# Branch products in three terms of rounded operands, in a mixer and mixture-of-experts kernel

## The chip, the cores and the metric

The kernel runs on one core of one Trainium2 chip. The metric is the device time of one execution in microseconds, the median of several runs. TensorE (PE) multiplies matrices, VectorE (DVE), ScalarE (ACT) and GpSimd (POOL) work on elements, SyncE (SP) issues most transfers. Each engine takes its instructions in the order written; between engines semaphores order the work.

## The reference

One layer for 512 tokens of width 1024. The input goes through one wide projection into four attention branches of four heads (A forgetting, B sliding window, C differential, D dilated) and into four gates of width 1024. The mixer's output is, cut to what matters:

```
for i, y in enumerate((ya, yb, yc, yd)):          # each [512, 256]
    merged = merged + sigmoid(gates[:, :, i]) * (y @ w_branch[i])
return merged @ w_out
```

Branch C is normalised by its mean square over each head before that. Behind the mixer come a layer norm, a router that picks 8 of 64 experts for a token, the experts and a shared one, and a second layer norm. All arrays are float32.

## The kernel before

**Stages.** First the projections and the attention, then mixing (`w_out`), router, 64 experts one after another with weights streamed from memory, and the sum. The change lies in the first stage, which ends near 496 us. SyncE issues the loads of all that follows (`x_nat`, the shared and the experts' weights) only after the last branch product and the last addition, since their memory is that of the attention.

**Rounded operands.** A large product is made of three: every operand is split in a high part, rounded to the type float32r by a ScalarE copy, and a low part, the remainder (GpSimd or VectorE subtracts). The product is high x high + high x low + low x high, all float32r. The branch products alone, of those in this stage with a large weight, use plain float32.

**Weights.** They come in chunks through a ring of three slots (`chunk`, L494 on): 22 chunks of eight 128x128 blocks for projections, then 32 chunks of ten blocks, one for each merge step: eight for a piece of the gate, two of `w_branch`. `split(n)` of ScalarE (L1053) copies the eight gate blocks of chunk n to `w_hi`, `split(n)` of GpSimd (L1649) makes `w_lo`; both have two buffers. SyncE waits, before it loads a slot again, for the remainder of a projection's chunk, or for the branch product of a merge's chunk, as that product reads the slot.

**A merge step m** (32 of them, eight to a branch, one for each 128 columns of the output): `part` 3m to 3m+2 are the three terms of the gate product, each eight matmuls of 128x512 (L680). `gate` is ScalarE's tanh of it (L1130); behind it in ScalarE's queue stands the split of chunk 22+m+2. `branch` is the branch product (L789), two float32 matmuls from `w` in the ring and the turned output `yT`. `gated` is VectorE's (tanh + 1) x product (L1386), and GpSimd adds it to `mT` (L1672).

**The order** of the work is one list, made by `order_of_work`, that every engine walks through. Attention steps (scores, bias, exponential, transpose, values) stand between the parts of merge steps: two steps in each of merges 0 to 5 and 14 to 21, four in each of merges 6 to 13, of branch C. Merges 22 to 31 have none between. In the first kind the list reads `part part, step, part gate branch, step, gated`, in the second `part, step, part, step, part gate, step, branch, step, gated`.

**Turned outputs.** When the last step of a branch is done, `turn_y` (two for a branch, L769) transposes its output on TensorE, and ScalarE copies it to `yT` with a factor of one half (L1124). For branch C the output is first normalised: VectorE's sums (L1349 to L1352), a root on GpSimd (`root`, L1647), VectorE's scaling (`norm_c`, L1362). GpSimd's root stands in its queue behind its split in merge 15. Transposes take two banks in turn, and wait for the copy out of the bank two before.

**w_out**, 4 MB, goes over the first 8192 elements of `region1`. It is issued after chunk 48, whose own wait is for 24 branch products.

```
elif kind == "branch":                              # TensorE
    w = ring[:, j % RING, :].rearrange("p (c n) -> p c n", c=10)
    for c in range(2):
        mm = nc.tensor.matmul(PS[:, C_BANK + 1, :], w[:, KT + c, :], yT[:, (br % 2) * 2 + c, :], ...)
```

Of the kernel before, what the change touches and what calls it, by code (L numbers as in the profile page):

```python
# [26 lines left out]
F32 = mybir.dt.float32  # L27
# [178 lines left out]
def build(nc, a, out):  # L206
# [9 lines left out]
    with ctx:  # L216
# [55 lines left out]

        x_hi = sb1("x_hi", [P, KT, SEQ], F32R)
        x_lo = sb1("x_lo", [P, KT, SEQ], F32R)
        w_hi = sb1("w_hi", [P, HALVES, KT, P], F32R)
        w_lo = sb1("w_lo", [P, HALVES, KT, P], F32R)
        ring = sb1("ring", [P, RING, SLOT])
        region1 = sb1("region1", [P, 29190])

        def carve(region, start, shape):  # L280
            n = int(np.prod(shape))
# [17 lines left out]
        kD, o = carve(region1, o, (2, SEQ))  # L299
        V, o = carve(region1, o, (QT, 7, P))  # L300
        probs, o = carve(region1, o, (3, SEQ + 2))
        probsT, o = carve(region1, o, (3, SEQ))
        Y, o = carve(region1, o, (2 * QT, F))
        yT, o = carve(region1, o, (4, SEQ))
        gate, o = carve(region1, o, (2, SEQ))
        gated, o = carve(region1, o, (2, SEQ))
        assert o == 29190, o
# [20 lines left out]
        for b in range(2):  # L328
            landing = ExitStack()
            raw[b] = landing.enter_context(nc.sbuf_tensor(f"raw{b}", [P, GU + DN], F32))  # L330
            landing.close()
            w_lo_e[b] = sb(f"w_lo_e{b}", [P, GU + DN], F32R)
            if b == 0:

                first = ExitStack()
                first.enter_context(nc.sbuf_tensor("x_nat_from", [P, GU + DN - QT * D], F32))
# [76 lines left out]
        yc_stat = sem("yc_stat")  # L413
        yc_rms = sem("yc_rms")
        y_ready = sem("y_ready")
        gate_done = sem("gate_done")
        gate_tanh = sem("gate_tanh")
        branch_done = sem("branch_done")
# [71 lines left out]
        def _(sp):  # L490
            def chunk(j):
                if j >= RING:

                    if j - RING < N_PROJ:  # L494
                        sp.wait_ge(w_lo_made, j - RING + 1)
                    else:
                        sp.wait_ge(branch_done, j - RING - N_PROJ + 1)
                src, n = (a["w_proj"][j], KT * P) if j < N_PROJ else (a["w_merge"][j - N_PROJ], 10 * P)
                sp.dma_start(ring[:, j % RING, 0:n], src).then_inc(ring_in[j % RING], 16)

# [43 lines left out]
            for j in range(12, N_CHUNKS):  # L544
                chunk(j)
                if j == W_OUT_AFTER:

                    sp.wait_ge(scores_done, last_step[BR_C] + 1)
                    sp.dma_start(w_out, a["w_out"][0].rearrange("(k p) n -> p k n", p=P)).then_inc(w_out_in, 16)


# [85 lines left out]
        def _(pe):  # L637
# [47 lines left out]
            def x_product(bank, n):  # L685
# [10 lines left out]
                    mm = x_product_part(bank, n, i)  # L696
                return mm

            for kind, n in order:
                if kind == "proj":  # L700
                    u = n
# [23 lines left out]
                elif kind == "turn":  # L725
                    u = turn_at[kind, n]
                    br, _, _, qt = STEPS[n]
                    if br == BR_C:
                        pe.wait_ge(combined, (n - FIRST_C) // 2 + 1)
                    else:  # L730
                        pe.wait_ge(probs_made, n + 1)
                    if u >= 2:
                        pe.wait_ge(turned_out, u - 1)
                    else:
                        pe.wait_ge(forget_exp, 1)
                    for j in range(keys_of(br, qt)[1]):
                        mm = nc.tensor.transpose(PS[:, T_BANK + u % 2, j * P:(j + 1) * P],  # L737
                                                 probs[:, n % 3, j * P:(j + 1) * P], ident[:, :])
                    mm.then_inc(turned, 1)
                elif kind == "turn_v":  # L740
                    u = turn_at[kind, n]
                    pe.wait_ge(proj_out, n + 1)
                    if u >= 2:
                        pe.wait_ge(turned_out, u - 1)
                    else:
                        pe.wait_ge(forget_exp, 1)
                    for t in range(QT):
                        mm = nc.tensor.transpose(PS[:, T_BANK + u % 2, t * P:(t + 1) * P],
                                                 vT[:, V_AT[PROJ[n][1:]] % 2, t * P:(t + 1) * P], ident[:, :])
                    mm.then_inc(turned, 1)  # L750
                elif kind == "values":
                    br, _, _, qt = STEPS[n]
                    k0, nk = keys_of(br, qt)
                    need = max(m for m, x in enumerate(PROJ) if x[1] == br and x[0] == "v")
                    pe.wait_ge(turned_out, max(turn_at["turn", n], turn_at["turn_v", need]) + 1)
                    v = VALUE_AT[n]
                    if v >= 2:
                        pe.wait_ge(y_made, v - 1)
                    for j in range(nk):
                        mm = nc.tensor.matmul(PS[:, O_BANK + v % 2, 0:HD], probsT[:, v % 3, j * P:(j + 1) * P],  # L760
                                              v_of(n, k0 + j), start=(j == 0), stop=(j == nk - 1))
                    mm.then_inc(values_done, 1)
                elif kind == "turn_y":
                    u = turn_at[kind, n]
                    br, j = n // 2, n % 2
                    pe.wait_ge(y_ready, br + 1)
                    pe.wait_ge(turned_out, u - 1)
                    for t in range(QT):
                        mm = nc.tensor.transpose(PS[:, T_BANK + u % 2, t * P:(t + 1) * P],  # L769
                                                 Y[:, (br % 2) * QT + t, j * P:(j + 1) * P], ident[:, :])  # L770
                    mm.then_inc(turned, 1)
                elif kind == "part":
                    m, i = divmod(n, 3)
                    if i == 0:
                        if m == 0:
                            pe.wait_ge(proj_out, N_PROJ)
                        else:
                            pe.wait_ge(gate_tanh, m)
                    mm = x_product_part(C_BANK, N_PROJ + m, i)
                    if i == 2:  # L780
                        mm.then_inc(gate_done, 1)
                elif kind == "branch":
                    j, br = N_PROJ + n, n // KT
                    w = ring[:, j % RING, :].rearrange("p (c n) -> p c n", c=10)
                    pe.wait_ge(turned_out, turn_at["turn_y", 2 * br + 1] + 1)
                    if n >= 1:
                        pe.wait_ge(gated_made, n)
                    for c in range(2):
                        mm = nc.tensor.matmul(PS[:, C_BANK + 1, :], w[:, KT + c, :], yT[:, (br % 2) * 2 + c, :],  # L789
                                              start=(c == 0), stop=(c == 1))  # L790
                    mm.then_inc(branch_done, 1)


# [19 lines left out]
            def turn_x1(t):  # L813
                pe.wait_ge(x1_made, t + 1)
                if t == 0:
                    pe.wait_ge(turned_out, len(turns))
                else:
                    pe.wait_ge(x1T_made, t)
                xs = x1[:, t, :].rearrange("p (q c) -> p c q", c=KT)
# [225 lines left out]
        def _(act):  # L1045
# [7 lines left out]
            def split(n):  # L1053

                if n < N_CHUNKS:
                    act.wait_ge(ring_in[n % RING], 16 * (n // RING + 1))
                    nc.scalar.activation(w_hi[:, n % HALVES, :, :],  # L1057
                                         ring[:, n % RING, 0:KT * P].rearrange("p (c n) -> p c n", c=KT), ACT.Copy)\
                        .then_inc(w_hi_made, 1)

            split(0)
# [13 lines left out]
            for kind, n in order:  # L1075
# [42 lines left out]
                elif kind == "turn_y":  # L1118
# [5 lines left out]
                    nc.scalar.activation(yT[:, (br % 2) * 2 + j, :], PS[:, T_BANK + u % 2, :], ACT.Copy, scale=0.5)\  # L1124
                        .then_inc(turned_out, 1)
                elif kind == "gate":
                    act.wait_ge(gate_done, n + 1)
                    if n >= 2:
                        act.wait_ge(gated_made, n - 1)
                    nc.scalar.activation(gate[:, n % 2, :], PS[:, C_BANK, :], ACT.Tanh, scale=0.5)\  # L1130
                        .then_inc(gate_tanh, 1)
                    split(N_PROJ + n + HALVES)

            def x1T_copy(t):
# [115 lines left out]
        def _(dve):  # L1250
# [117 lines left out]
            for kind, n in order:  # L1368
# [3 lines left out]
                        norm_c()  # L1372
                elif kind == "join":
                    combine(n)
                elif kind == "values":
                    out_step(n)
                elif kind == "gated":
# [244 lines left out]
        def _(pool):  # L1622
# [25 lines left out]

            def split(n):  # L1649

                w = ring[:, n % RING, 0:KT * P].rearrange("p (c n) -> p c n", c=KT)
                wh, wl = w_hi[:, n % HALVES, :, :], w_lo[:, n % HALVES, :, :]
# [134 lines left out]
```

## Time and profile before

| | us |
|---|---|
| median of 3 runs (lowest to highest) | 1338.59 (1338.19 to 1339.23) |
| the profiled execution, its own time | 1335.51 |
| its span in the profile | 1333.9 |
| TensorE busy | 1265.3 (95%) |
| VectorE busy | 779.1 (58%) |
| ScalarE busy | 706.6 (53%) |
| GpSimd busy | 386.9 (29%) |
| mean TensorE clock granted | 0.981 of full |

The span is the time from the first to the last instruction in the profile; the profiled execution's own time holds a little around it, and it is 3 us under the median of the runs. A busy share is a mean over stages that are limited by different things. The end of a matmul is modelled and matmuls overlap, so their price is read from starts: where one group starts and where the next one does.

### The profile page before, as it was taken

How to read it: one execution, taken by the hardware profiler on the slowest of the kernel's cores; microseconds unless marked ns; L12 is line 12 of the kernel's file. 1: busy time of each engine (PE TensorE's matmuls, PEld its weight loads, DVE VectorE, ACT ScalarE, POOL GpSimd, SP SyncE). 2: the span in 40 equal slices, each digit the busy share in tenths (PEclk: the TensorE clock that was granted, in tenths of full speed). 3: DMA queues.
4: the chain of work that ended last, by engine and by line, in shares of the span. 5: the costliest groups of instructions: out<-in, count | busy, mean ns of one | idle time of the engine just before them, and what ended most of it. 6: DMA issues, size and time to landing. Idle time of an engine off the chain costs nothing.

```text
span 1333.9 us, 14628 instructions
## 1 busy us (share of the span) xinstructions
PE 1265.3 (95%) x5488; PEld 919.0 (69%) x5488; DVE 779.1 (58%) x1071; ACT 706.6 (53%) x854; POOL 386.9 (29%) x262
## 2 busy tenths in 40 slices
PE   7999999999999999969999999999999999999965
PEld 4888866566667764444887777777777777777722
DVE  4011122344422014642888888888888888887858
ACT  4333433333333210011778888887888888887710
POOL 3433322223333430253332322223223223233201
PEclk9999999999999999979999999999999999999978
DMA  4922112111112515042899999999999999999686
GB/s 160 324 85 80 59 45 74 40 59 60 40 66 73 205 43 226 1 159 82 323 378 380 373 367 374 370 376 357 363 375 375 368 361 375 363 370 371 250 333 250
DMA packets 68118, 311.28 MB, mean 233 GB/s; under 512 B 17788, under 2 KB 17916, under 8 KB 41552
## 3 DMA queue, kind: packets, MB, share of 16 engines
q1 hardware_dynamic: 48560, 276.64, 56.0%
q0 software_dynamic: 19488, 33.70, 6.7%
q8 instruction: 45, 0.74, 0.2%
q14 instruction: 25, 0.20, 0.0%
HBM read 305.74 MB, written 42.01 MB: 261 GB/s over the span
## 4 chain that ended last, share of the span: by engine, by line
PE 61%; DMA 25%; ACT 5%; DVE 5%; issue 2%; POOL 1%; another core or an unknown queue 1%; SPq 0%; POOLq 0%; DVEq 0%; ACTq 0%
DMA raw<-in_w_gu 23%; PE PS L680 22%; PE PS L926 8%; PE PS L789 4%; PE PS L876 4%; ACT w_hi_e L1156 4%; PE PS L723 4%; PE PS L879 3%; PE PS L873 3%; PE PS L807 3%; PE PS L760 2%; PE PS L737 2%; DMA parts<-y_d 1%; PE PS L858 1%; PE PS L907 1%
## 5 line engine op out<-in xcount | busy, mean ns | idle before, releaser
L1475 DVE TENSOR_TENSOR w_lo_e<-raw,w_hi_e 128x2048 fp32r<-128x2048 f32 x192 | 433.8, 2283 | 5.0 <-ACT w_hi_e L1156 5.0
L1156 ACT ACTIVATE w_hi_e<-raw 128x2048 fp32r<-128x2048 f32 x192 | 368.4, 1920 | 111.6 <-DMA raw<-in_w_gu 70.0
L1703 POOL DMA_INDIRECT y_d<-y_slots,tab x64 | 113.6, 1776 | 425.6 <-PE PS L945 305.8
L1655 POOL TENSOR_TENSOR w_lo<-ring,w_hi 128x1024 fp32r<-128x1024 f32 x54 | 128.3, 2376 | 309.3 <-ACT w_hi L1057 309.3
L1318 DVE CUSTOM_DVE_ANT_0 region<-PS,region 128x128 f32<-128x128 f32 (+3 forms) x64 | 31.4, 491 | 211.6 <-PE PS L723 210.1
L876 PE MATMUL PS<-w_hi_e,xs_lo 128*128 128x512 f32 x512 | 144.5, 404 | 0.0
L873 PE MATMUL PS<-w_hi_e,xs_hi 128*128 128x512 f32 x512 | 143.8, 402 | 0.0
L879 PE MATMUL PS<-w_lo_e,xs_hi 128*128 128x512 f32 x512 | 138.7, 393 | 0.0
L1100 ACT ACTIVATE region<-region,nmax 128x128 f32<-128x128 f32 (+5 forms) x80 | 43.6, 545 | 139.8 <-DVE nmax L1318 139.6
L876 PEld LDWEIGHTS PS<-w_hi_e,xs_lo 128*128 128x128 f32 x512 | 91.7, 188 | 33.4 <-DVE xs_lo L1501 16.0
L680 PE MATMUL PS<-x_hi,w_hi 128*128 128x512 f32 x424 | 112.8, 408 | 0.0
L879 PEld LDWEIGHTS PS<-w_lo_e,xs_hi 128*128 128x128 f32 x512 | 96.1, 188 | 22.3
L680 PE MATMUL PS<-x_hi,w_lo 128*128 128x512 f32 x432 | 110.4, 398 | 0.0
L680 PE MATMUL PS<-x_lo,w_hi 128*128 128x512 f32 x424 | 105.7, 391 | 0.0
L873 PEld LDWEIGHTS PS<-w_hi_e,xs_hi 128*128 128x128 f32 x512 | 91.5, 189 | 15.6 <-issue 0.5
L680 PEld LDWEIGHTS PS<-x_hi,w_lo 128*128 128x128 f32 x432 | 80.4, 190 | 16.0
L680 PEld LDWEIGHTS PS<-x_lo,w_hi 128*128 128x128 f32 x424 | 79.0, 188 | 16.4
L680 PEld LDWEIGHTS PS<-x_hi,w_hi 128*128 128x128 f32 x424 | 76.8, 189 | 18.1 <-issue 4.1
L926 PE MATMUL PS<-w_hi_e,hT_hi 128*128 128x512 f32 x256 | 75.2, 415 | 11.5 <-ACT hT_hi L1174 8.2
L1698 POOL DMA_INDIRECT x_slots<-x_d,tab x64 | 71.6, 1120 | 49.7 <-PE PS L945 28.8
L1501 DVE TENSOR_TENSOR xs_lo<-PS,xs_hi 128x1024 fp32r<-128x1024 f32 x64 | 77.9, 1218 | 3.8 <-ACT xs_hi L1180 3.8
L1496 DVE TENSOR_TENSOR hT_lo<-PS,hT_hi 128x256 fp32r<-128x256 f32 x64 | 27.1, 424 | 81.9 <-ACT hT_hi L1174 81.8
(177 smaller groups left out, 1695.3 us busy)
## 6 DMA issues: line engine op xcount, KB each, us to landing
raw<-in_w_gu SPq DMA_DIRECT2D x128, 1024.0 KB, 11.6
raw<-in_w_down_e SPq DMA_DIRECT2D x64, 1024.0 KB
ring<-in_w_merge SPq DMA_DIRECT2D x32, 640.0 KB, 3.9
ring<-in_w_proj SPq DMA_DIRECT2D x22, 512.0 KB, 3.5
parts<-y_d SPq DMA_DIRECT2D x8, 1024.0 KB, 15.9
parts<-y_d SPq DMA_DIRECT2D x4, 1536.0 KB, 12.8
region<-in_w_out SPq DMA_DIRECT2D x1, 4096.0 KB, 16.3
bias_d<-bias_rows SPq DMA_DIRECT2D x3, 1280.0 KB, 11.4
```

The source lines that it names most:

```text
L680: mm = nc.tensor.matmul(PS[:, bank, :], (w_hi, w_hi, w_lo)[i][:, n % HALVES, c, :], (x_hi, x_lo, x_hi)[i][:, c, :], start=(i == 0 and c == 0),
L723: nc.tensor.matmul(PS[:, S_BANK + n % 2, 0:nk * P], q, k, start=True, stop=True)\
L873: nc.tensor.matmul(to, xs_hi[:, b, c, :], wh[:, c, :], start=(c == 0), stop=False)
L876: nc.tensor.matmul(to, xs_lo[:, b, c, :], wh[:, c, :], start=False, stop=False)
L879: mm = nc.tensor.matmul(to, xs_hi[:, b, c, :], wl[:, c, :], start=False, stop=(c == KT - 1))
L926: mm = nc.tensor.matmul(PS[:, Y_BANK + n, :], hx[:, s % 2, half, :], w[:, half, n * 512:(n + 1) * 512], start=(first and half == 0), stop= ...
L1156: nc.scalar.activation(w_hi_e[b][:, lo:hi], raw[b][:, lo:hi], ACT.Copy).then_inc(made, 1)
L1475: nc.vector.tensor_tensor(w_lo_e[b][:, lo:hi], raw[b][:, lo:hi], w_hi_e[b][:, lo:hi].bitcast(F32), ALU.subtract).then_inc(made, 1)
L1501: nc.vector.tensor_tensor(xs_lo[:, e % 2, :, :], PS[:, X_BANK:X_BANK + 2, :].rearrange("p a (c n) -> p (a c) n", n=P), xs_hi[:, e % 2, :, ...
L1655: nc.gpsimd.tensor_tensor(wl, w, wh.bitcast(F32), ALU.subtract).then_inc(w_lo_made, 1)
L1698: pool.indirect_dma_start(x_slots[:, b, :], None, x1_d, bass.IndirectOffsetOnAxis(ap=rows, axis=0), bounds_check=last_tok, oob_is_err=Fals ...
L1703: pool.indirect_dma_start(y_d, bass.IndirectOffsetOnAxis(ap=rows, axis=0), y_slots[:, b, :], None, bounds_check=last_row, oob_is_err=False ...
```

## The change

The branch product is made as the others are, from three terms of rounded operands.

- Both splits take all ten blocks of a merge's chunk, so `w_hi` and `w_lo` have ten blocks to a buffer.
- ScalarE's copy of the turned output goes to `yT_hi`, rounded. VectorE makes the remainder `yT_lo` from the same bank, a new instruction at each of the eight `turn_y`, with waits for the memory it is put over. `yT_lo` lies where q of branch A or a strip of bias lay.
- TensorE has six matmuls for two. The third term waits for the remainders. Transposes whose bank held a turned output wait for VectorE's remainder too (`turn_bank_free`).
- The split of chunk 22+m+2 now overwrites what branch product m reads. So it moves in ScalarE's queue from behind the tanh of gate m to the place of branch m in the list, and waits for that branch product. GpSimd's split keeps its place and waits for ScalarE's as before.
- A ring slot is loaded again once GpSimd has made the remainders of its chunk, for all chunks. `w_out` gets a wait of its own for 24 branch products.
- `region1` grows by 2 elements, and `x_nat` lies over another buffer.

```
         w_hi = sb1("w_hi", [P, HALVES, SLOT // P, P], F32R)          # was KT
         w_lo = sb1("w_lo", [P, HALVES, SLOT // P, P], F32R)
+        yT_hi = in_region1("yT_hi", Y_AT + 2 * QT * F, [P, 4, SEQ])
+        yT_lo = [in_region1(f"yT_lo{b}", at, [P, 2, SEQ]) for b, at in enumerate((0, 8192))]
...
 # SyncE
             def chunk(j):
                 if j >= RING:
-                    if j - RING < N_PROJ:
-                        sp.wait_ge(w_lo_made, j - RING + 1)
-                    else:
-                        sp.wait_ge(branch_done, j - RING - N_PROJ + 1)
+                    sp.wait_ge(w_lo_made, j - RING + 1)
...
                     sp.wait_ge(scores_done, last_step[BR_C] + 1)
+                    sp.wait_ge(branch_done, 3 * KT)
                     sp.dma_start(w_out, ...)
...
 # TensorE
+            def turn_bank_free(u):
+                if u >= 2:
+                    pe.wait_ge(turned_out, u - 1)
+                    if turns[u - 2][0] == "turn_y":
+                        pe.wait_ge(yT_lo_made, turns[u - 2][1] + 1)
+                else:
+                    pe.wait_ge(forget_exp, 1)
...
                 elif kind == "branch":
-                    j, br = N_PROJ + n, n // KT
-                    w = ring[:, j % RING, :].rearrange("p (c n) -> p c n", c=10)
+                    b, br = (N_PROJ + n) % HALVES, n // KT
                     pe.wait_ge(turned_out, turn_at["turn_y", 2 * br + 1] + 1)
                     if n >= 1:
                         pe.wait_ge(gated_made, n)
-                    for c in range(2):
-                        mm = nc.tensor.matmul(PS[:, C_BANK + 1, :], w[:, KT + c, :], yT[:, (br % 2) * 2 + c, :],
-                                              start=(c == 0), stop=(c == 1))
+                    y_hi, y_lo = yT_hi[:, (br % 2) * 2:(br % 2) * 2 + 2, :], yT_lo[br % 2]
+                    for i, (w, y) in enumerate(((w_hi, y_hi), (w_lo, y_hi), (w_hi, y_lo))):
+                        if i == 2:
+                            pe.wait_ge(yT_lo_made, 2 * br + 2)
+                        for c in range(2):
+                            mm = nc.tensor.matmul(PS[:, C_BANK + 1, :], w[:, b, KT + c, :], y[:, c, :],
+                                                  start=(i == 0 and c == 0), stop=(i == 2 and c == 1))
                     mm.then_inc(branch_done, 1)
...
 # ScalarE
                 if n < N_CHUNKS:
                     act.wait_ge(ring_in[n % RING], 16 * (n // RING + 1))
-                    nc.scalar.activation(w_hi[:, n % HALVES, :, :],
-                                         ring[:, n % RING, 0:KT * P].rearrange("p (c n) -> p c n", c=KT), ACT.Copy)\
+                    k = KT if n < N_PROJ else SLOT // P
+                    nc.scalar.activation(w_hi[:, n % HALVES, 0:k, :],
+                                         ring[:, n % RING, 0:k * P].rearrange("p (c n) -> p c n", c=k), ACT.Copy)\
                         .then_inc(w_hi_made, 1)
...
                     nc.scalar.activation(gate[:, n % 2, :], PS[:, C_BANK, :], ACT.Tanh, scale=0.5)\
                         .then_inc(gate_tanh, 1)
+                elif kind == "branch":
+                    act.wait_ge(branch_done, n + 1)
                     split(N_PROJ + n + HALVES)
...
 # VectorE
+                elif kind == "turn_y":
+                    u = turn_at[kind, n]
+                    br, j = n // 2, n % 2
+                    dve.wait_ge(turned_out, u + 1)
+                    if br == BR_A:
+                        dve.wait_ge(scores_done, last_step[BR_A] + 1)
+                    elif br == BR_B:
+                        dve.wait_ge(biased, last_step[BR_B] + 1)
+                    else:
+                        dve.wait_ge(branch_done, (br - 1) * KT)
+                    nc.vector.scalar_tensor_tensor(yT_lo[br % 2][:, j, :], PS[:, T_BANK + u % 2, :], 0.5,
+                                                   yT_hi[:, (br % 2) * 2 + j, :].bitcast(F32), ALU.mult, ALU.subtract)\
+                        .then_inc(yT_lo_made, 1)
...
 # GpSimd, split(n)
-                w = ring[:, n % RING, 0:KT * P].rearrange("p (c n) -> p c n", c=KT)
+                k = KT if n < N_PROJ else SLOT // P
+                w = ring[:, n % RING, 0:k * P].rearrange("p (c n) -> p c n", c=k)
```

## Rows read from the trace of the kernel before

**Rows 1.** The page: busy time of each engine; TensorE's granted clock in 40 slices.
```profile
PE 1265.3 (95%) x5488; PEld 919.0 (69%) x5488; DVE 779.1 (58%) x1071; ACT 706.6 (53%) x854; POOL 386.9 (29%) x262
...
PEclk9999999999999999979999999999999999999978
```

**Rows 2.** TensorE's waits, whole span: line, releaser, us in total, times, longest.
```profile
PE PS L691 <- ACT x_hi L1065: 6.5, 1, 6.5
...
PE PS L769 <- ACT region L1110: 2.5, 2, 1.8
...
PE PS L769 <- DVEq L1366: 1.5, 1, 1.5
...
PE PS L737 <- ACT region L1110: 0.5, 1, 0.5
PE PS L737 <- ACT region L1100: 0.2, 1, 0.2
```

**Rows 3.** Chain of waits in order of time: start us, us, what.
```profile
176.65 1.72 PE PS L789 x4
...
474.71 5.46 PE PS L680 x24
```

**Rows 4.** Timeline of a late merge step: start us, us, engine, line, operation.
```profile
472.83 1.88 PE L789 MATMUL PS<-region,ring 128*128 128x512 f32 x4
...
473.52 1.05 ACT L1057 ACTIVATE w_hi<-ring 128x1024 fp32r<-128x1024 f32 x1
...
474.65 2.40 POOL L1655 TENSOR_TENSOR w_lo<-ring,w_hi 128x1024 fp32r<-128x1024 f32 x1 [3.73 <-ACT w_hi L1057]
474.80 0.69 DVE L1386 SCALAR_TENSOR_TENSOR region<-region,PS 128x512 f32<-128x512 f32 x1 [6.49 <-PE PS L789]
...
476.38 1.98 PE L680 MATMUL PS<-x_lo,w_hi 128*128 128x512 f32 x8
...
478.19 1.98 PE L680 MATMUL PS<-x_hi,w_lo 128*128 128x512 f32 x8
...
480.00 1.88 PE L789 MATMUL PS<-region,ring 128*128 128x512 f32 x4
```

**Rows 5.** Timeline of an early merge step, TensorE (L723 are scores).
```profile
181.39 1.98 PE L680 MATMUL PS<-x_lo,w_hi 128*128 128x512 f32 x8
183.30 0.70 PE L723 MATMUL PS<-region 64*128 64x256 f32 x2
...
186.28 1.88 PE L789 MATMUL PS<-region,ring 128*128 128x512 f32 x4
...
188.09 0.70 PE L723 MATMUL PS<-region 64*128 64x256 f32 x2
```

**Rows 6.** Timeline around the normalisation of branch C.
```profile
347.70 1.88 PE L789 MATMUL PS<-region,ring 128*128 128x512 f32 x4
...
349.52 2.35 POOL L1655 TENSOR_TENSOR w_lo<-ring,w_hi 128x1024 fp32r<-128x1024 f32 x1 [7.45 <-ACT w_hi L1057]
...
349.70 2.21 DVE L1352 TENSOR_SCALAR yc_ss<-yc_ss 128x16 f32<-128x16 f32 x1
...
352.04 2.94 POOL L1647 TENSOR_TENSOR yc_ss<-yc_ss,half_neg 128x16 f32<-128x16 f32 x1 [0.17 <-DVEq L1353]
...
355.01 3.22 DVE L1362 SCALAR_TENSOR_TENSOR region<-region,yc_ss,norm_g 128x64 f32<-128x64 f32 x16 [1.80 <-POOL yc_ss L1647]
...
358.34 0.66 PE L769 MATMUL PS<-ident,region 128*128 128x128 f32 x4 [1.50 <-DVEq L1366]
...
361.56 3.22 PE L680 MATMUL PS<-x_hi,w_lo 128*128 128x512 f32 x8
```

**Rows 7.** Stretches: us, busy by engine, granted TensorE clock, DMA share, GB/s.
```profile
362.00:363.00 1.00, 1.00 (x4) 0.71 (x4) 0.00 (x0) 0.54 (x1) 0.00 (x0) 0.50 0.00 0
```

**Rows 8.** Timeline: `w_out` issued, and ScalarE's split of chunk 49.
```profile
438.34 0.96 SPq L549 DMA_DIRECT2D region<-in_w_out  x1
...
456.26 1.06 ACT L1057 ACTIVATE w_hi<-ring 128x1024 fp32r<-128x1024 f32 x1 [4.16 <-DMA ring<-in_w_merge]
```

More of the change, by code:

```diff
@@ L274, in build, with in_region1 @@
         x_lo = sb1("x_lo", [P, KT, SEQ], F32R)
-        w_hi = sb1("w_hi", [P, HALVES, KT, P], F32R)
-        w_lo = sb1("w_lo", [P, HALVES, KT, P], F32R)
+        w_hi = sb1("w_hi", [P, HALVES, SLOT // P, P], F32R)
+        w_lo = sb1("w_lo", [P, HALVES, SLOT // P, P], F32R)
         ring = sb1("ring", [P, RING, SLOT])
-        region1 = sb1("region1", [P, 29190])
+        Y_AT = 23048
+        def in_region1(name, at, shape):
+            with ExitStack() as own:
+                if at:
+                    own.enter_context(nc.sbuf_tensor(name + "_from", [P, at], F32))
+                return own.enter_context(nc.sbuf_tensor(name, shape, F32R))
+        yT_hi = in_region1("yT_hi", Y_AT + 2 * QT * F, [P, 4, SEQ])
+        yT_lo = [in_region1(f"yT_lo{b}", at, [P, 2, SEQ]) for b, at in enumerate((0, 8192))]
+        region1 = sb1("region1", [P, 29192])
         def carve(region, start, shape):
@@ L301, in build @@
         probs, o = carve(region1, o, (3, SEQ + 2))
-        probsT, o = carve(region1, o, (3, SEQ))
+        probsT, o = carve(region1, o + 2, (3, SEQ))
         Y, o = carve(region1, o, (2 * QT, F))
+        y_hi_at = o
         yT, o = carve(region1, o, (4, SEQ))
@@ L306, in build @@
         gated, o = carve(region1, o, (2, SEQ))
-        assert o == 29190, o
+        assert o == 29192, o
+        assert y_hi_at == Y_AT + 2 * QT * F, y_hi_at
         fg = yT[0:4, :, :]
@@ L332, in build @@
             w_lo_e[b] = sb(f"w_lo_e{b}", [P, GU + DN], F32R)
-            if b == 0:
+            if b == 1:
                 first = ExitStack()
-                first.enter_context(nc.sbuf_tensor("x_nat_from", [P, GU + DN - QT * D], F32))
                 x_nat = first.enter_context(nc.sbuf_tensor("x_nat", [P, QT, D], F32))
@@ L415, in build @@
         y_ready = sem("y_ready")
+        yT_lo_made = sem("yT_lo_made")
         gate_done = sem("gate_done")
@@ L731, in _ @@
                         pe.wait_ge(probs_made, n + 1)
[L732 to L735, printed above, removed]
+                    turn_bank_free(u)
                     for j in range(keys_of(br, qt)[1]):
@@ L742, in _ @@
                     pe.wait_ge(proj_out, n + 1)
[L743 to L746, printed above, removed]
+                    turn_bank_free(u)
                     for t in range(QT):
@@ L766, in _ @@
                     pe.wait_ge(y_ready, br + 1)
-                    pe.wait_ge(turned_out, u - 1)
+                    turn_bank_free(u)
                     for t in range(QT):
@@ L816, in turn_x1 @@
                     pe.wait_ge(turned_out, len(turns))
+                    pe.wait_ge(yT_lo_made, 8)
                 else:
@@ L1123, in _ @@
                         act.wait_ge(branch_done, (br - 1) * KT)
-                    nc.scalar.activation(yT[:, (br % 2) * 2 + j, :], PS[:, T_BANK + u % 2, :], ACT.Copy, scale=0.5)\
+                    nc.scalar.activation(yT_hi[:, (br % 2) * 2 + j, :], PS[:, T_BANK + u % 2, :], ACT.Copy, scale=0.5)\
                         .then_inc(turned_out, 1)
@@ L1649, in split @@
             def split(n):
-                w = ring[:, n % RING, 0:KT * P].rearrange("p (c n) -> p c n", c=KT)
-                wh, wl = w_hi[:, n % HALVES, :, :], w_lo[:, n % HALVES, :, :]
+                k = KT if n < N_PROJ else SLOT // P
+                w = ring[:, n % RING, 0:k * P].rearrange("p (c n) -> p c n", c=k)
+                wh, wl = w_hi[:, n % HALVES, 0:k, :], w_lo[:, n % HALVES, 0:k, :]
                 pool.wait_ge(w_hi_made, n + 1)
```

## The prediction

> **What bounds the kernel now.** I read the page first: TensorE is busy for 95% of the span, at its full clock nearly everywhere [rows 1]. Then the list of TensorE's waits over the whole span: before 520 us, where all edits lie, it waited at the start (L691), 0.7 us in two waits before transposes (L737) and at L769, the transposes of a finished branch output; nowhere did the gate or branch products of a merge step wait [rows 2]. Then the chain of waits: from 100 to 496 us it runs almost wholly through TensorE, in pieces of 24 gate matmuls (5.46 us) and of the branch product (1.72 us) [rows 3]. So in this stage a microsecond of TensorE is a microsecond of the kernel, except around 350 us, where the chain leaves TensorE for GpSimd and VectorE. Last the timeline of single merge steps, for prices. What follows the stage (mixing, router, experts) hangs on its last branch product and on nothing earlier, so its start moves and its length does not: the loads of the expert stage too are issued only behind that point.
>
> **The branch product: the gain.** Before, two float32 matmuls of 128x512, each recorded as two, make a branch product. In the last ten merge steps one step is a period of 7.17 us (472.83 to 480.00). A group of eight rounded matmuls is 1.81 us from start to start (476.38 to 478.19), so 24 are 5.43 and the branch product 7.17 - 5.43 = 1.74 us [rows 4]. Afterwards it is six rounded matmuls of the same size, all with 128 weight columns: 6 x 1.81 / 8 = 1.36 us. Gain 0.38; with the chain's prices (1.72, and 6 x 5.46 / 24 = 1.365) 0.355 [rows 3]. I take 0.37, and 10 x 0.37 = 3.7 us.
>
> In the other 22 steps attention scores follow the branch product. There it takes 1.81 us to the start of the scores (186.28 to 188.09); eight rounded matmuls take 1.91 to that point (181.39 to 183.30), 0.10 over their 1.81, so six take 1.36 + 0.10 = 1.46 [rows 5]. Gain 0.35; 21 x 0.35 = 7.35 us. The twenty-second is merge 15, below. Together 11.05 us. Ends: 0.33 and 0.38 for each of 31, so 10.2 to 11.8. That four records become six pairs of load and matmul costs nothing further: the loads of rounded groups lie beside the matmuls in the 1.81.
>
> **The moved split (ScalarE, GpSimd).** The high parts of the weights for merge m+2 were made right behind the tanh of gate m, beside branch product m; now they wait for its end. ScalarE runs 1.05 us for eight blocks, GpSimd 2.40 [rows 4]; ten blocks are at most 10/8 of it, 1.31 and 3.0 us. The next engine starts about 0.23 us behind the last matmul: VectorE's product comes 474.80 - 472.83 = 1.97 us after the start of a branch product of 1.74 [rows 4]. GpSimd follows ScalarE by 474.65 - (473.52 + 1.05) = 0.08. So behind branch m the split is whole at 0.23 + 1.31 + 0.08 + 3.0 = 4.6 us. High parts are wanted one merge later (5.43 + 1.36 = 6.8 us), low parts 3.6 us behind that. Both fit; GpSimd's 3.0 and its one addition of 128x512 for a merge (half the elements of the old split, so about 1.2) stay under 6.8. Cost 0.
>
> Behind ScalarE's new wait stand the exponential of the following step, its copies of transposed probabilities, and then the next tanh. The exponential comes about 1.3 us behind the branch product anyway, since scores and VectorE's bias come first, and the wait and split take 1.5: late by 0.2 to 0.5 us. TensorE wants its result only after 8 to 16 gate matmuls (1.8 to 3.6 us). Cost 0, ends 0 and 0.3 for a step (a rival, below). In the last steps nothing stands behind it but the next tanh, 5.4 us later.
>
> **The place where the split is late.** The normalisation of branch C runs VectorE sums, a GpSimd root, VectorE scaling, then the transposes of L769. GpSimd has the root queued behind the split for merge 17. Before: GpSimd's split 349.52 to 351.87, VectorE's sums ended at 351.91, so the two arrive together and the root starts at 352.04 [rows 6]. Now the split waits for branch 15, started at 347.70: 347.70 + 1.36 + 0.23 = 349.29 for ScalarE, 350.60 its end, GpSimd 350.68 to 353.68, root 353.74. That is 1.7 us later than 352.04. Everything behind is one chain (root 2.94, scaling 3.2, transposes at 358.34), and TensorE already waits 1.5 us there for it [rows 2, 6], so 1.7 us goes in full on the path, and merge 15's own gain is lost in the wait. Ends: 1.3 (if ten blocks cost less than 10/8 on both engines) and 2.2.
>
> The clock: behind this pause it is at 1.2 GHz (0.50 granted) [rows 7], and the eight matmuls of 361.56 are recorded at 3.22 us against 1.98 for a warm group [rows 4, 6]. The pause now is about 2 us longer (1.7 + 0.35). I put 0.3 us on it; ends 0 and 1.7 (another group like this one, 3.22 - 1.98 = 1.24, and a third more for transposes and branch product).
>
> **VectorE's remainders and the transposes.** Eight scalar_tensor_tensor of 128x512 from PSUM: 0.69 us each by the nearest row, VectorE's product for a merge [rows 4], 5.5 us in all, on an engine that TensorE waits for nowhere in the merge steps but at the place above [rows 2]. Three pairs stand before a branch product with 8 to 24 gate matmuls between. For branch C only eight stand between; at the low clock these take 3 us, while a copy of 0.6 and a remainder of 0.69 follow the last transpose, and the remainder is wanted only by the third pair of matmuls. The next two transposes (waiting now for the remainder too) come a group of gate matmuls later. Cost 0, ends 0 and 0.5 for all four branches. ScalarE's copies are what they were.
>
> **Ring slots, w_out, x_nat.** Weights of a merge are now loaded when GpSimd has split the earlier ones: the slot is free sooner, gain nothing since no product waited for one. w_out still waits for 24 branch products. But chunk 49, which was issued a merge later, now goes right behind the 4 MB. w_out was issued at 438.34 and ScalarE got chunk 49 at 456.26, 17.9 us later [rows 8]. The queue holds the same bytes, so I keep 17.9. ScalarE wants it at about 452.5 in the same count, gets it at 456.2, ends at 457.5; the tanh behind it is wanted at 457.9, the high parts at 459.0. Cost 0 with 0.4 us of slack; if chunk 50, now in the queue too, is served with it (640 KB beside 4096 and 640, 17.9 x 640 / 4736 = 2.4 us), 2.0 us. x_nat changes its place, not its time.
>
> **Sum.** 11.05 - 1.7 - 0.3 = 9.05, say 9.1 us. The profiled execution took 1335.5 us (span 1333.9), so 1326.4 for one like it; the median of the runs is 3.1 above it, and 1338.6 - 9.1 = 1329.5.
>
> **The rivals.** *Full gain (0.10):* the late root is hidden, because ten blocks cost scarcely more than eight, or the order on GpSimd leaves room. For it: root and split arrived within 0.04 us of each other, against it that TensorE waited there already. 11.4 us: 1327.2.
>
> *The clock takes more (0.16):* a longer pause at 357 to 362 us makes a longer stretch at 1.2 GHz. For it: the clock fell there already after pauses of 1.5 and 1.8 us; against: it was back after eight matmuls. One more such stretch costs 1.7 us, two 3.4: gain 5.7 to 7.4, 1332. The Trainium skill (TensorE: Matmul & The Clock Gate, "HAM oscillation") has the rule that a wait between groups of matmuls makes the next group start at the low clock, each time anew; the trace agrees, with 0.50 granted behind this pause [rows 7]. By that rule only this place would pay, since no other merge has a pause.
>
> *Stalls from the ring (0.06):* behind w_out the tanh comes late for several merges, 0.8 to 3 us. 1331.5.
>
> *The wait on ScalarE decides (0.04), the slower end:* if the exponential, held by wait and split (1.5 us), reached TensorE in each of the 22 steps with attention, 22 x 1.5 - 9.1 = 24 us would be lost: 1362. It decides from 9.1 / 22 = 0.41 us for each step on. Against it: 1.8 to 3.6 us of matmuls lie between, and not one wait for an exponential stands in the merge steps now [rows 2]. Partly true (0.1 to 0.4 a step) it gives no change: 0.04 more, 1337.
>
> *No gain from rounding (0.03):* six matmuls do not stream at the rate of the gate's groups, because operand pairs change every two. At 0.29 us each nothing is gained: 1338.6 + 2.
>
> **The numbers.** Forecast 0.57; full gain 0.10, clock 0.16, ring 0.06, ScalarE 0.04 in full and 0.04 in part, no gain 0.03. The forecast's own range, from 10.2 and 11.8 with 1.3 to 2.2 for the root and 0 to 0.8 for clock and ring together, is a gain of 7.2 to 10.5; the range reaches to the full gain with its upper price (12) and to the clock's rival: 1326.8 to 1333.2. A measurement of this kernel tells about 0.2% (2.7 us) from no change. Faster by more: 0.57 + 0.10 + 0.16 + 0.06 = 0.89; within it 0.04 + 0.03 = 0.07; slower 0.04.
>
> **What would show it.** L789 with 192 records at a start-to-start of 0.23 us; a period of 6.8 us in the last ten merges; ScalarE's split 0.2 us behind each branch product; GpSimd's split at 3.0; the root starting right behind a split and not behind VectorE, the transposes of branch C 1.7 us later against branch 15; mixing starting about 9 us earlier and the expert stage as long as before. Wrong would be: waits of TensorE at L737 in the merge steps, a period over 7 us, or a low clock after 370 us.

## The result and the profile after

The changed kernel took 1326.5 us in the median of 4 runs (1324.7 to 1327.7), the kernel before 1338.4 (1337.9 to 1339.2): ratio 0.9909, interval 0.9892 to 0.9926. That is 11.9 us less by the medians and 12.2 by the ratio (9.9 to 14.5). The range began at 1326.8, so the time lies just outside it, by 0.3 us. Repeated with more runs (c1 and e1 below) the ratio was 0.9924 and 0.9922: 10.1 and 10.4 us; the changed kernel took 1327.4 us there, inside the range, and 1326.5, and the kernel before 1337.4 and 1337.2. The two profiled executions, 1335.5 and 1327.7 us, are only 7.8 apart: the first was 2.9 us faster than the median of its kernel, the second the slowest of its four. The three intervals overlap, so the gain is about 10 us, and what the first comparison shows above that can be scatter.

The page of the changed kernel, for rows 1:

```profile
PE 1255.2 (95%) x5552; PEld 931.0 (70%) x5552; DVE 793.9 (60%) x1079; ACT 715.9 (54%) x854; POOL 406.6 (31%) x262
...
PEclk9999999999899999979999999999999999999978
```

Its list of TensorE's waits, for rows 2 (L702 was L691, L782 was L769, L753 was L737; the gate's matmuls are now L691, and were L680). There is still no wait of a gate or branch product of a merge step. The wait for the scaling of branch C has grown from 1.5 to 3.3 us:

```profile
PE PS L702 <- ACT x_hi L1083: 6.8, 1, 6.8
PE PS L782 <- DVEq L1387: 3.3, 1, 3.3
PE PS L782 <- ACT region L1128: 2.1, 2, 1.4
...
PE PS L753 <- ACT region L1128: 0.6, 1, 0.6
```

The timeline of a late merge step, for rows 4 (start us, us, engine):

```profile
466.41 0.63 PE L805 MATMUL PS<-yT_hi,w_hi 128*128 128x512 f32 x2
...
466.87 0.63 PE L805 MATMUL PS<-yT_hi,w_lo 128*128 128x512 f32 x2
...
467.34 0.63 PE L805 MATMUL PS<-yT_lo,w_hi 128*128 128x512 f32 x2
...
467.81 2.00 PE L691 MATMUL PS<-x_hi,w_hi 128*128 128x512 f32 x8
468.01 1.28 ACT L1075 ACTIVATE w_hi<-ring 128x1280 fp32r<-128x1280 f32 x1 [0.80 <-PE PS L805]
468.07 0.69 DVE L1421 SCALAR_TENSOR_TENSOR region<-region,PS 128x512 f32<-128x512 f32 x1 [6.18 <-PE PS L805]
469.36 2.95 POOL L1691 TENSOR_TENSOR w_lo<-ring,w_hi 128x1280 fp32r<-128x1280 f32 x1 [2.66 <-ACT w_hi L1075]
469.65 1.98 PE L691 MATMUL PS<-x_lo,w_hi 128*128 128x512 f32 x8
...
473.27 0.63 PE L805 MATMUL PS<-yT_hi,w_hi 128*128 128x512 f32 x2
```

The period is 473.27 - 466.41 = 6.86 us; the branch product is 1.40 from its start to the gate's. A pair comes every 0.465 us, not 0.453, and the eight gate matmuls behind them take 469.65 - 467.81 = 1.84 us, not 1.81. ScalarE's split starts 0.20 us behind the start of the gate's matmuls, which is where the branch product ends; GpSimd's is whole 4.5 us behind that point, for 4.6 as worked out. Early, with scores behind (rows 5), 176.95 to 178.44 is 1.49 us:

```profile
176.95 0.63 PE L805 MATMUL PS<-yT_hi,w_hi 128*128 128x512 f32 x2
...
178.44 0.70 PE L742 MATMUL PS<-region 64*128 64x256 f32 x2
```

The normalisation of branch C, for rows 6:

```profile
343.42 0.63 PE L805 MATMUL PS<-yT_hi,w_hi 128*128 128x512 f32 x2
...
345.02 1.27 ACT L1075 ACTIVATE w_hi<-ring 128x1280 fp32r<-128x1280 f32 x1 [0.80 <-PE PS L805]
345.42 0.17 DVE L1373 TENSOR_SCALAR yc_ss<-yc_ss 128x16 f32<-128x16 f32 x1
...
346.37 2.95 POOL L1691 TENSOR_TENSOR w_lo<-ring,w_hi 128x1280 fp32r<-128x1280 f32 x1 [6.34 <-ACT w_hi L1075]
...
349.28 2.94 POOL L1682 TENSOR_TENSOR yc_ss<-yc_ss,half_neg 128x16 f32<-128x16 f32 x1
...
352.25 3.22 DVE L1383 SCALAR_TENSOR_TENSOR region<-region,yc_ss,norm_g 128x64 f32<-128x64 f32 x16 [5.01 <-POOL yc_ss L1682]
...
355.58 1.12 PE L782 MATMUL PS<-ident,region 128*128 128x128 f32 x4 [3.33 <-DVEq L1387]
```

VectorE's sums are ready at 345.59, and the root starts 3.7 us later, right behind the split. From branch 15 to the transposes it is 12.16 us; before it was 10.64 [rows 6]. The clock at this place (the third figure from the end is the granted share), before and then changed:

```profile
360.60:364.00 3.40, 3.18 (x10) 2.73 (x11) 0.00 (x0) 1.16 (x3) 0.02 (x1) 0.50 0.02 5
```
```profile
354.60:361.40 6.80, 4.46 (x14) 3.61 (x15) 3.87 (x14) 2.06 (x5) 1.26 (x1) 0.50 0.00 0
```

**Where the time went.** Each kernel's execution cut at the first start of five kinds of matmul, in us: branch product, mixing, shared expert, routed experts, then the last start of these, and the end. Low: stretches of 3.4 us at 0.5 granted clock that lie in mixing.

| kernel | branch to mixing | mixing to shared (low) | shared to experts | experts | rest |
|---|---|---|---|---|---|
| before | 319.6 | 70.9 (2) | 68.4 | 624.2 | 74.4 |
| changed | 311.5 | 69.2 (1) | 68.3 | 626.0 | 74.0 |
| c1 changed, again | 311.3 | 69.2 (1) | 68.3 | 623.8 | 73.9 |
| e1 changed, again | 311.4 | 69.2 (1) | 68.2 | 623.4 | 74.0 |
| c2 root first | 310.7 | 69.2 (1) | 68.4 | 624.4 | 73.9 |
| c3 late split alone | 322.1 | 69.2 (1) | 71.0 | 625.8 | 74.6 |
| c4 x_nat alone | 319.7 | 70.9 (2) | 68.5 | 627.1 | 74.5 |
| d1 root first, quiet | 307.8 | 67.5 (0) | 59.6 | 625.4 | 74.4 |
| e2 the same, again | 307.9 | 67.5 (0) | 70.3 | 623.5 | 74.1 |
| d2 before, root quiet | 316.1 | 70.9 (2) | 57.6 | 626.6 | 74.6 |
| d3 two terms | 296.9 | 69.2 (1) | 57.9 | 625.7 | 74.0 |
| d4 twelve matmuls | 356.2 | 69.2 (1) | 59.6 | 623.6 | 74.0 |

The attention stage repeats within 0.2 us; it gained 8.1 to 8.3. Mixing gained 1.6, of which the prediction knew nothing. Together 9.7 to 9.9, near the 10.1 and 10.4 of the repeats. The experts take 623.4 to 627.1 us whatever the kernel, and 623.4 to 626.0 in three executions of the changed one. That is wide enough to hold the 2 us left between these sums and the first comparison; that they lay there is not shown, for in the traces of that comparison the changed kernel's experts took 1.8 us longer, not shorter.

### The profile page after: what moved, and what is told of

The parts are those of the page before. It is cut to its first block, busy times and chain, and to the rows that moved or that the text cites. A ratio compares the mean times of both kernels' runs of the same rounds, so it can differ in the third digit from the quotient of the medians.

```text
span 1326.0 us, 14804 instructions
## 1 busy us (share of the span) xinstructions
PE 1255.2 (95%) x5552; PEld 931.0 (70%) x5552; DVE 793.9 (60%) x1079; ACT 715.9 (54%) x854; POOL 406.6 (31%) x262
## 4 chain that ended last, share of the span: by engine, by line
PE 58%; DMA 24%; issue 5%; ACT 5%; DVE 3%; POOL 3%; another core or an unknown queue 1%; SPq 0%; POOLq 0%; DVEq 0%; ACTq 0%
DMA raw<-in_w_gu 22%; PE PS L691 19%; PE PS L943 9%; PE PS L823 4%; PE PS L893 4%; PE PS L896 4%; PE PS L890 4%; ACT w_hi_e L1177 4%; PE PS L805 3%; PE PS L742 2%; POOL w_lo L1691 2%; PE PS L773 2%; DMA parts<-y_d 1%; PE PS L875 1%; PE PS L753 1%
## 5 line engine op out<-in xcount | busy, mean ns | idle before, releaser
L1691 POOL TENSOR_TENSOR w_lo<-ring,w_hi 128x1280 fp32r<-128x1280 f32 (+1 forms) x54 | 146.8, 2720 | 295.1 <-ACT w_hi L1075 295.1
L691 PE MATMUL PS<-x_hi,w_lo 128*128 128x512 f32 x432 | 110.5, 398 | 0.0
L691 PE MATMUL PS<-x_hi,w_hi 128*128 128x512 f32 x424 | 109.6, 400 | 0.0
L691 PE MATMUL PS<-x_lo,w_hi 128*128 128x512 f32 x424 | 105.8, 392 | 0.0
L691 PEld LDWEIGHTS PS<-x_hi,w_lo 128*128 128x128 f32 x432 | 80.5, 190 | 16.0
L691 PEld LDWEIGHTS PS<-x_lo,w_hi 128*128 128x128 f32 x424 | 79.0, 188 | 16.4
L691 PEld LDWEIGHTS PS<-x_hi,w_hi 128*128 128x128 f32 x424 | 76.8, 189 | 15.0 <-issue 0.2
L943 PE MATMUL PS<-w_hi_e,hT_hi 128*128 128x512 f32 x256 | 75.6, 417 | 11.9 <-ACT hT_hi L1195 9.2
L1734 POOL DMA_INDIRECT x_slots<-x_d,tab x64 | 68.0, 1062 | 49.6 <-PE PS L962 28.8
L1075 ACT ACTIVATE w_hi<-ring 128x1280 fp32r<-128x1280 f32 (+1 forms) x54 | 63.8, 1181 | 33.3 <-PE PS L805 25.1
```

The source lines that it names most:

```text
L691: mm = nc.tensor.matmul(PS[:, bank, :], (w_hi, w_hi, w_lo)[i][:, n % HALVES, c, :], (x_hi, x_lo, x_hi)[i][:, c, :], start=(i == 0 and c == 0),
L943: mm = nc.tensor.matmul(PS[:, Y_BANK + n, :], hx[:, s % 2, half, :], w[:, half, n * 512:(n + 1) * 512], start=(first and half == 0), stop= ...
L1075: nc.scalar.activation(w_hi[:, n % HALVES, 0:k, :], ring[:, n % RING, 0:k * P].rearrange("p (c n) -> p c n", c=k), ACT.Copy)\
L1734: pool.indirect_dma_start(x_slots[:, b, :], None, x1_d, bass.IndirectOffsetOnAxis(ap=rows, axis=0), bounds_check=last_tok, oob_is_err=Fals ...
```

## The experiments

**c1, e1: the changed kernel again.** No edit.

> The changed kernel once more, timed in five rounds with the kernel before, to tell the stage prices from scatter. Theory A (the gain is that of the attention stage alone, 8.1 us in the two traces, and the 3.8 us between it and the 11.9 us of the medians are scatter of the stages behind): gain 7.5 to 9.5 us over five rounds. Theory B (the later stages are really shorter in the changed kernel): gain 11 to 13 us, and the profile shows less than 838 us from the first mixing matmul to the end.

> The changed kernel a third time, beside e2 on one chip. By the traces so far the gain over the kernel before is 8.2 us in the attention stage and 1.6 us in mixing, where the kernel before meets two stretches of low clock and the changed one one: 9.8 us. If the 11.9 us of the first comparison were the true size, the gain would be over 11 us again.

Ratio 0.9924 (0.9911 to 0.9937) and 0.9922 (0.9908 to 0.9935), each in 6 runs against 23 and 11 of before. By their middle values neither theory of c1's expectation held: the gain is above 9.5 us and below 11. The intervals (8.4 to 11.9 us, and 8.7 to 12.3) rule out neither by themselves; the traces do, since theory A left out the 1.6 us of mixing and theory B asks for more than all stages together gained. From the first mixing matmul to the end c1 took 835.2 us, but the changed kernel's first profile 837.6, so the 838 told nothing; the table's second column does.

**c4: x_nat alone.** The kernel before:

```
-            if b == 0:
+            if b == 1:
                 first = ExitStack()
-                first.enter_context(nc.sbuf_tensor("x_nat_from", ...))
```

> The kernel before with only x_nat over the other buffer. Theory A (the place is of no effect, the later stages only scatter): within 0.5 us of before. Theory B (its place shortens the stages behind mixing): 3 to 4 us faster, and from the first mixing matmul to the end 834 us instead of 837.8.

Ratio 1.0002 (0.9991 to 1.0014), mixing 70.9 as before, and 840.9 us from the first mixing matmul to the end: its place has no effect that the runs show.

**c3: the late split alone.** The kernel before with ten-block splits, ScalarE's behind the branch product, as in the change; float32 branch product.

```
                         .then_inc(gate_tanh, 1)
+                elif kind == "branch":
+                    act.wait_ge(branch_done, n + 1)
                     split(N_PROJ + n + HALVES)
```

> The kernel before, float32 branch product, with only the split changed: ten blocks, behind the branch product, waiting for it (and x_nat over the other buffer, which the larger tiles need). Theory A (late split costs only at the root, where before GpSimd was busy until 351.87): 1.7 to 2.2 us slower than before, all of it between merge 15 and 16, periods of 7.17 us as before. Rival (ScalarE's wait costs in each merge): the same stretch from first branch product to mixing is over 3 us longer.

Ratio 1.0017 (1.0008 to 1.0027), the stretch 2.5 us longer. The period of late merge steps is 7.17 us, and no wait of TensorE in a merge step was added, but the one for the scaling is as in the changed kernel:

```profile
PE PS L768 <- DVEq L1369: 3.3, 1, 3.3
```

From branch 15 to branch 16 it takes 2.3 us more than before: 1.8 up to the transposes, and 0.5 behind them, where the low clock now lasts 6.8 us. So ScalarE's wait costs nothing to speak of in the merges, and the split costs at the root, 0.3 us more than expected. With the three terms on top (changed against c3) the stretch falls by 10.6 us.

**c2: root first.** The changed kernel, GpSimd:

```
+                if m == merges_before_norm:
+                    root(yc_ss[:, :], yc_stat, 1, yc_rms)
                 if N_PROJ + m + HALVES < N_CHUNKS:
                     split(N_PROJ + m + HALVES)
-                if m == merges_before_norm:
-                    root(yc_ss[:, :], yc_stat, 1, yc_rms)
```

> The changed kernel, with GpSimd's root for branch C put ahead of its split in merge 15. Theory A (the whole wait of 3.3 us before the transposes comes from the root standing behind the late split, and the low clock from that wait): the transposes are not late, the granted clock stays at 1.0, TensorE's L782 waits fall from 5.4 us to under 1.5, gain over the changed kernel 4 to 6 us. Rival: TensorE waits for sums, root and scaling anyway as in the kernel before (1.5 us and the low clock): gain only 1.5 us.

Only 0.7 us less in the stretch, and no gain in the whole (ratio to before 0.9925, as c1). The timeline of c2 says why:

```profile
345.28 2.94 POOL L1682 TENSOR_TENSOR yc_ss<-yc_ss,half_neg 128x16 f32<-128x16 f32 x1 [5.69 <-DVEq L1374]
...
348.17 2.95 POOL L1691 TENSOR_TENSOR w_lo<-ring,w_hi 128x1280 fp32r<-128x1280 f32 x1
...
348.25 5.89 DVE L1383 SCALAR_TENSOR_TENSOR region<-region,yc_ss,norm_g 128x64 f32<-128x64 f32 x16 [1.45 <-POOL yc_ss L1682]
```

The root is early, but GpSimd's split now runs beside VectorE's scaling, and that takes 5.89 us instead of 3.22. Both expectations failed: a second wait had been hidden behind the first.

**d1, e2: root first, split held.** As c2, and one line more:

```
                 if m == merges_before_norm:
                     root(yc_ss[:, :], yc_stat, 1, yc_rms)
+                    pool.wait_ge(y_ready, BR_C + 1)
```

> The changed kernel with GpSimd's root ahead of its split in merge 15, and that split held until VectorE has scaled branch C. In c2 the split ran beside the scaling, and 16 small operations took 5.89 us instead of 3.22. Theory A (GpSimd's split and VectorE's small operations hold each other up, and everything TensorE waits for there is late by that): scaling 3.2 us, transposes within 0.5 us of TensorE's arrival, no low clock at 352 to 359, and the stretch from first branch product to mixing 3 to 5 us under the 311.5 us of the changed kernel. Rival (another wait takes its place, the copy of turned probabilities): 1.5 us or less.

> The changed kernel with the root first and the split held, as d1, on the chip of e1. By the traces 3.7 us less in the attention stage and 1.6 us less in mixing (no low clock met there): 3.5 to 5.5 us faster than e1, 13 to 15 us faster than the kernel before. Rival (the low clock in mixing falls as it likes): 2 to 4 us faster than e1.

The timeline of d1:

```profile
346.02 2.94 POOL L1682 TENSOR_TENSOR yc_ss<-yc_ss,half_neg 128x16 f32<-128x16 f32 x1 [5.69 <-DVEq L1374]
...
348.99 3.22 DVE L1383 SCALAR_TENSOR_TENSOR region<-region,yc_ss,norm_g 128x64 f32<-128x64 f32 x16 [1.45 <-POOL yc_ss L1682]
...
352.35 2.90 POOL L1691 TENSOR_TENSOR w_lo<-ring,w_hi 128x1280 fp32r<-128x1280 f32 x1 [3.39 <-DVEq L1387]
...
352.39 0.60 PE L782 MATMUL PS<-ident,region 128*128 128x128 f32 x4
...
354.80 0.63 PE L782 MATMUL PS<-ident,region 128*128 128x128 f32 x4 [1.81 <-ACT region L1128]
355.19 3.50 PE L691 MATMUL PS<-x_hi,w_lo 128*128 128x512 f32 x8
```

The wait for the scaling is gone. The second pair of transposes still waits 1.8 us for the copy of turned probabilities, and the eight matmuls behind still ran at the low clock, against the expectation. The stretch is 3.5 to 3.6 us shorter than in the changed kernel, mixing 1.7 (no low stretch in it). On one chip e2 took 1322.6 us and e1 1326.5, before 1337.2: ratio to before 0.9887 (0.9870 to 0.9904); d1's was 0.9895 (0.9879 to 0.9910). This version beats both kernels. The 4.0 us between e1 and e2 lie in both ranges of e2's expectation and decide nothing between them; what speaks for its first theory is that mixing again took 67.5 us without a low stretch.

**d2: the same edits in the kernel before.**

> The kernel before with the same two edits at the root. Theory A: there GpSimd's split and the root meet as well (VectorE's last sum took 2.21 us beside it, 0.17 in the changed kernel), so this one gains too, 2 to 3 us from first branch product to mixing (319.6 before); against d1 the difference is the branch products alone, 32 x 0.30 to 0.32 = 9.9 us. Rival (the arrival of sums and split was accidental and the wait is the root's own length): under 1 us.

Its timeline:

```profile
349.46 0.17 DVE L1352 TENSOR_SCALAR yc_ss<-yc_ss 128x16 f32<-128x16 f32 x1
349.77 2.94 POOL L1647 TENSOR_TENSOR yc_ss<-yc_ss,half_neg 128x16 f32<-128x16 f32 x1 [7.93 <-DVEq L1353]
...
356.44 0.61 PE L769 MATMUL PS<-ident,region 128*128 128x128 f32 x4
...
358.93 2.09 PE L680 MATMUL PS<-x_hi,w_lo 128*128 128x512 f32 x8
```

Ratio 0.9976 (0.9965 to 0.9987), the stretch 3.5 us shorter, more than the 2 to 3 expected. The meeting of sums and split in the kernel before was no accident: VectorE's last sum took 2.21 us there and ended with GpSimd's split [rows 6], and 0.17 here and in the changed kernel, where no split ran beside it. The transposes come 1.7 us earlier against branch 15; the other 1.8 us are behind them, where the low clock of the kernel before is gone and the copy is waited for 1.5 us instead of 1.8. Against d1 the stretch is 8.2 us longer, and d1 has a low stretch at branch C that d2 has not (worth about 1.7 us, an estimate from the clock's halving of 3.4), so the branch products alone give some 9.9 us, 0.31 each.

**d3: two terms.** The third term of the branch products is left out (four matmuls).

```
-                    for i, (w, y) in enumerate(((w_hi, y_hi), (w_lo, y_hi), (w_hi, y_lo))):
-                        if i == 2:
+                    for i, (w, y) in enumerate(((w_hi, y_hi), (w_lo, y_hi))):
+                        if i == 1:
```

> The changed kernel without the third term of the branch products (high weights x low outputs): four matmuls for six. Theory A (attention stage bound by TensorE's columns): 31 x 0.47 = 14.6 us less from first branch product to mixing, about 297. Beyond mixing theory C (low-clock stretches stand at fixed times of the execution and meet mixing or not) lets mixing and router take 69.2 or 70.8 us, or another value, without a change of their code; the rival, that they depend on the kernel, gives 69.2 again.

The kernel took 1300.6 us, ratio to before 0.9806 (0.9790 to 0.9822). 14.6 us less in the stretch, as worked out: TensorE bounds the stage. Mixing took 69.2 us, as the rival said.

**d4: twelve matmuls.** The term high weights x low outputs four times.

```
+                    for i, (w, y) in enumerate(((w_hi, y_hi), (w_lo, y_hi), (w_hi, y_lo), (w_hi, y_lo), (w_hi, y_lo), (w_hi, y_lo))):
```

> The changed kernel with the third term issued four times, twelve matmuls for six (the sums then hold that term four times). Theory A (each matmul costs 0.235 us in this place because of its operands): 32 x 1.41 = 45 us more from first branch product to mixing. Rival (0.235 is a passing cost of about 0.06 us at the start of a branch product, and further ones cost 0.227): 32 x 1.36 = 43.6 us more. Theory C gives mixing and router lengths other than 69.2 us here too, the rival 69.2.

The kernel took 1361.9 us, ratio to before 1.0273 (1.0254 to 1.0291). The stretch grew by 44.8 us, between the two and nearer to theory A. Of this 1.8 us lie between branches 15 and 16; a step with scores grew by about 1.39 us. A late merge step of d4:

```profile
505.29 0.63 PE L805 MATMUL PS<-yT_hi,w_hi 128*128 128x512 f32 x2
505.76 0.63 PE L805 MATMUL PS<-yT_hi,w_lo 128*128 128x512 f32 x2
506.23 2.01 PE L805 MATMUL PS<-yT_lo,w_hi 128*128 128x512 f32 x8
508.08 1.98 PE L691 MATMUL PS<-x_hi,w_hi 128*128 128x512 f32 x8
509.89 1.98 PE L691 MATMUL PS<-x_lo,w_hi 128*128 128x512 f32 x8
```

The gate's first eight behind it are at 1.81 us again, where behind six matmuls they took 1.84. Its period is 513.52 - 505.29 = 8.23 us, 1.37 over 6.86, or 0.228 for each of six more. So in the late steps the slow pace belongs to the first dozen matmuls from the start of a branch product, and not to the operands of its own six: in the changed kernel the gate's first matmuls are among that dozen, in d4 the added ones. What makes it was not tried; ScalarE's tanh runs there. Mixing took 69.2 us, as the rival said, but with its low stretch at another place (below).

## Why the prediction was right or wrong

**Bound and direction: right.** TensorE's microseconds in the stage were the stage's, one for one (14.6 us for 14.6 in d3).

**The gain of a branch product: right mechanism, size too large.** 0.37 was taken in the last ten and 7.17 - 6.86 = 0.31 measured; 0.35 with scores behind and 1.81 - 1.49 = 0.32 measured in most of them. Six matmuls were priced at the pace of eight in the midst of a gate product, 0.227 us; at this place they come at 0.235, and the eight behind lose 0.03. The sum, 11.05, should have been 21 x 0.32 + 10 x 0.31 = 9.8.

**Moved split at no cost in the merges: right** (c3). ScalarE 1.27 and GpSimd 2.95 us for ten blocks, for 1.31 and 3.0.

**Late root: right in place, 1.5 for 1.7 us.** But the reading that sums and split "arrive together" took a hold-up for an arrival. The sum's row said 2.21 us for 128x16 elements; without the split beside it it takes 0.17 (d2). Read so, it would have pointed to GpSimd and VectorE standing in each other's way here, where both kernels had some 3.5 us to gain (d1, d2).

**Clock at this place:** low for 6.8 us where it was 3.4, as the clock's rival had it, but it began at 354.6, in the wait, and ran through the transposes and the wait for the copy, in which TensorE did little. From the transposes of branch C to branch product 16 it took 361.95 - 355.58 = 6.37 us, 6.27 before: 0.1 for the 0.3 put on it; the wait for the copy fell from 1.8 to 1.4 us in the same span.

**Remainders, x_nat, ring: right at nothing.** c4 shows it for x_nat. ScalarE got chunk 49 at 447.96, 15.1 us behind `w_out` at 432.87, where 17.9 were kept; it waited 1.35 us for it and TensorE for nothing.

**The range's own ends.** The text reaches to a gain of 12 us, which from 1338.6 gives 1326.6; the range was put at 1326.8. The time of 1326.5 is outside either. And "a low clock after 370 us" could not be a sign of being wrong as it is worded: the kernel before has low stretches in mixing itself, at 527.8 and 558.6.

**The step that failed** is in the first part: "so its start moves and its length does not". The start of mixing moved by 8.1 us against the first branch product, and mixing became 1.6 us shorter. The timelines of 32 of its matmuls, first before and then changed:

```profile
527.58 15.65 PE L807 MATMUL PS<-region,mT 128*128 128x512 f32 x32
```
```profile
519.99 13.95 PE L823 MATMUL PS<-region,mT 128*128 128x512 f32 x32
```

The same 32 matmuls, behind the same pause of TensorE (it waits 1.2 us for ScalarE's copy before the router's matmuls, which stand ahead of these). The granted clock of these stretches, before and then changed:

```profile
527.80:531.20 3.40, 3.40 (x5) 1.38 (x5) 3.23 (x14) 0.20 (x1) 0.00 (x0) 0.51 0.27 110
```
```profile
520.00:534.00 14.00, 14.00 (x37) 6.35 (x37) 7.68 (x35) 0.23 (x1) 0.00 (x0) 1.00 0.09 37
```

Before, the clock was at 1.2 GHz for 3.4 us; in the changed kernel it stayed at 2.4. With the branch products at 9.8, the root at -1.5 and the clock at -0.1 the stage gives 8.2, and 1.6 from mixing makes 9.8: the predicted 9.1 was near by luck, by two errors of opposite sign. Taken from 1338.6, 9.8 us would give 1328.8, within the range; the 2.3 us from there to 1326.5 are not explained by any stage. The median of the kernel before was 1.0 to 1.2 us lower when it was repeated with more runs, the experts' stage scatters by up to 3.7 us, and the range had no term for either, since the median before was taken for exact.

Open is what decides whether a pause is followed by a low stretch. Mixing has three pauses of TensorE of 1.2 us, each ahead of a group of router matmuls, in every kernel, and each low stretch in mixing begins 1.7 to 2.3 us behind the end of one of them, and none elsewhere. In before, c4 and d2 it is behind the first and the third; in the three traces of the changed kernel, in c2 and d3 behind the third; in c3 and d4 behind the second; in d1 and e2 behind none. So the clock rival's rule, that each wait puts the next group at the low clock, does not hold here. Nor does the work of mixing decide it, since it is the same in all. The first theory of d3 and d4, that a shift in time changes what mixing meets, is not refuted by their 69.2 us: d4 had one low stretch like the changed kernel, but behind another pause. What differs is what comes ahead of mixing, and with it the time of its start: d1's edits end before it, and they took the last low stretch away. A kernel that was profiled again showed the same (the changed one in three traces, e2 as d1). Which start gives which pattern was not worked out, and no runs moved the start step by step.

## What to carry to other kernels

Price a matmul at the place where it will stand: the pace inside a long group is a lower bound for a short one. Where an engine's row is ten times longer than its like, look for the other engine that ran beside it; moving one of the two gave 3.5 us here in each kernel, but only when both collisions were removed (c2 against d1). A stage that starts at another time can meet other low stretches of the clock with the same code (mixing took 70.9, 69.2 or 67.5 us), and a range needs a term for that and for the scatter of the kernel before.

## What the runs showed of the hardware

- Small VectorE operations beside a GpSimd subtraction of 128x1280: 16 of them took 5.89 us instead of 3.22, and one of 128x16 took 2.21 instead of 0.17 beside one of 128x1024. The Trainium skill (GPSIMD Engine Reference, Specifications) has GpSimd share its SBUF interfaces with VectorE, with contention where a VectorE instruction has two SBUF inputs or runs in a two-port mode; the traces agree that there is contention, and give its price here. Which of the two cases the operation of 128x16 is, no trace shows.
- The same kernel before had a median of 1337.2 and 1337.4 us on two chips and 1326.0 on a third. The stretch from shared expert to routed ones took 68 to 71 us on the first two and 57.6 to 59.6 on the third, where TensorE's wait at L862 (L845 in the kernel before; positions for routing, on VectorE) was about 3 us and not 10.5 to 11.7. The kernel before was itself not profiled on the third; d1 to d4 were. What VectorE waited for there the profile does not name.
